# Ten expert slabs instead of eight, two of them on lent space

## The reference, cut to what matters

```python
h = layer_norm(ALPHA * h + mixed, ln_g[i, 0], ln_b[i, 0])
ffn = hierarchical_moe(h, ...)      # 32 experts, the best 2 per token
h = layer_norm(ALPHA * h + ffn, ln_g[i, 1], ln_b[i, 1])
# an expert: (silu(xb @ w_gate[e]) * (xb @ w_up[e])) @ w_down[e]
```

## Time and profile before

| what | us |
|---|---|
| median of 3 runs (2404.62 to 2407.61) | 2405.11 |
| the profiled execution's own time | 2405.83 |
| its span | 2404.1 |
| PE busy | 2144.1 (89%) |
| DVE busy | 736.6 (31%) |
| ACT busy | 515.1 (21%) |
| POOL busy | 301.3 (13%) |

### The profile page before, as it was taken

How to read it: one execution, slowest core, us unless ns; L and a number is a source line. 1 busy time by engine, 2 the same in 40 slices (tenths; PEclk the granted TensorE clock), 3 DMA queues, 4 the chain that set the end, 5 groups by cost and what they waited for, 6 DMA issues and landing times. The chain is left out here.

```text
span 2404.1 us, 28333 instructions
## 1 busy us (share of the span) xinstructions
PE 2144.1 (89%) x11502; PEld 1232.8 (51%) x11502; DVE 736.6 (31%) x1587; ACT 515.1 (21%) x1193; POOL 301.3 (13%) x309
## 2 busy tenths in 40 slices
PE   4999989999999999868999999959996899999991
PEld 2446644444444578345555455547754555455550
DVE  5054235342665445452111011042125211101104
ACT  1123221021554144212221121130001122112110
POOL 0000000212232211101111111022000111111101
PEclk9999988999999999978999999979997899999996
DMA  9315243042003121138999999971133899999992
GB/s 346 107 58 176 75 153 110 30 158 70 1 1 109 70 73 54 54 122 333 421 423 424 423 423 423 418 280 52 72 114 112 337 422 422 424 423 422 424 407 116
DMA packets 100567, 545.88 MB, mean 227 GB/s; under 512 B 13296, under 2 KB 27417, under 8 KB 66490
## 3 DMA queue, kind: packets, MB, share of 16 engines
q1 hardware_dynamic: 79238, 493.55, 50.8%
q0 software_dynamic: 20320, 48.01, 5.6%
q10 hardware_dynamic: 868, 2.38, 0.3%
HBM read 538.79 MB, written 28.94 MB: 236 GB/s over the span
## 5 line engine op out<-in xcount | busy, mean ns | idle before, releaser
L721 PE MATMUL ps<-arena,ring 128*128 128x512 f32 (+11 forms) x2000 | 608.0, 463 | 10.3 <-ACT arena L1349 3.0
L721 PEld LDWEIGHTS ps<-arena,ring 128*128 128x128 f32 (+3 forms) x2000 | 358.4, 190 | 247.7 <-issue 205.1
L1141 PE MATMUL ps<-ring,arena 128*64 128x256 f32 x3648 | 410.0, 382 | 2.3 <-DMA ring<-in_moe_w_up_dram 1.3
L1141 PEld LDWEIGHTS ps<-ring,arena 128*64 128x64 f32 x3648 | 257.5, 137 | 134.3 <-issue 3.0
L802 PE MATMUL ps<-ring,arena 128*128 128x512 f32 (+1 forms) x560 | 250.7, 605 | 6.5 <-DVE arena L2007 4.2
L1154 PE MATMUL ps<-ring,arena 128*64 128x512 f32 x896 | 210.8, 614 | 22.8 <-DMA ring<-in_moe_w_down_dram 22.8
L2157 DVE SCALAR_TENSOR_TENSOR arena<-arena,ps 128x256 f32<-128x256 f32 x78 | 32.9, 421 | 565.9 <-ACT arena L1541 565.9
L2417 POOL DMA_INDIRECT assignment_rows<-arena x78 | 82.1, 1052 | 827.4 <-ACT arena L1547 802.9
L802 PEld LDWEIGHTS ps<-ring,arena 128*128 128x128 f32 (+1 forms) x560 | 102.9, 187 | 141.3 <-issue 141.0
L1141 PE MATMUL ps<-arena 128*64 128x256 f32 x1344 | 151.1, 380 | 0.0
L1154 PEld LDWEIGHTS ps<-ring,arena 128*64 128x64 f32 x896 | 65.7, 142 | 135.6 <-issue 102.2
(11 more groups left out here) (299 smaller groups left out, 1826.2 us busy)
## 6 DMA issues: line engine op xcount, KB each, us to landing
ring<-in_moe_w_gate_dram SPq DMA_DIRECT2D x48, 2048.0 KB
ring<-in_moe_w_up_dram SPq DMA_DIRECT2D x48, 2048.0 KB
ring<-in_moe_w_down_dram SPq DMA_DIRECT2D x48, 2048.0 KB
arena<-in_moe_w_gate_dram SPq DMA_DIRECT2D x16, 2048.0 KB
arena<-in_moe_w_up_dram SPq DMA_DIRECT2D x16, 2048.0 KB
arena<-in_moe_w_down_dram SPq DMA_DIRECT2D x16, 2048.0 KB
ring<-in_ada_w_dram SPq DMA_DIRECT2D x12, 2048.0 KB
ring<-in_a_w_in_dram SPq DMA_DIRECT2D x12, 1536.0 KB
```

The lines of the kernel that those rows point to most:

```text
L721: ins = pe.matmul(dst, w, m, start=i == 0, stop=i == len(pairs) - 1)
L1141: ins = pe.matmul(ps[CAP * i:CAP * (i + 1), bank_, 256 * j:256 * (j + 1)], rows_t[:, k, :], w[:, k, 256 * i:256 * (i + 1)], start=k == 0, ...
```

## The change

Two more slab places, slots 8 and 9, are made out of the first 8192 columns of `arena`. These hold X (5120 columns), and the norm rows `lnp` (2048) and `gate_b` (1024) which are moved there; HT and all behind it move up by 3072 columns. The expert turns go round ten places instead of eight, starting with the ring, then HT's place, the mixer's, then slots 8 and 9. Turns of experts past position 22 skip slots 8 and 9; their last users are turn 58 (down of expert 18) and turn 59 (gate of expert 20). SP waits for `h_out` (X is in DRAM) ahead of turn 8.

X is read back from `h_rows` by POOL after scatter 30 (LENT_BACK is 30), 2.1 MB, followed by the gain and bias for alpha (1.05 MB). Alpha moves from the blocks 1 to 5 to the blocks 32 to 36 and waits for both reads (`x_lent`, `lnp_in`). The loads `load_lnp(2)` and `load_lnp(4)` ahead of the stages go away. The load of the next norm's rows moves from scatter 10 to behind scatter 38, the last one.

```diff
 RING = 6
-SLABS = 8
+SLABS = 10
 SLAB = 4096
+LENT = (8, 9)
+LAST_LENT = 22
...
-    for n, (kind, l, _) in enumerate(STREAM):
+    for n, (kind, l, at_) in enumerate(STREAM):
         if kind == "expert":
-            i = n - TURN[("expert", l, (0, 0))]
-            cycle = [(ring_at + j) % RING for j in range(RING)] + list(range(RING, SLABS))
-            s = cycle[i % SLABS]
+            if n == TURN[("expert", l, (0, 0))]:
+                cycle = deque([(ring_at + j) % RING for j in range(RING)] + list(range(RING, SLABS)))
+            while cycle[0] in LENT and at_[0] > LAST_LENT:
+                cycle.popleft()
+            s = cycle[0]
+            cycle.rotate(-1)
...
+LENT_BACK = sum(s <= LAST_LENT for s, _ in BLOCKS) + 1
...
-        arena = sb("arena", [P, 24576])
-        lnp = sb("lnp", [P, 2, D])
-        gate_b = sb("gate_b", [P, D])
+        arena = sb("arena", [P, 27648])
+        lnp = arena[:, 5120:7168].rearrange("p (i d) -> p i d", d=D)
+        gate_b = arena[:, 7168:8192]
...
-        HT = at(5120, DC * TM).rearrange("p (c t) -> p c t", t=TM)
-        R0 = 9344
+        HT = at(8192, DC * TM).rearrange("p (c t) -> p c t", t=TM)
+        R0 = 12416
...
-            return ring[:, s * SLAB:(s + 1) * SLAB] if s < RING else at((5120, R0 + 8192)[s - RING], SLAB)
+            return ring[:, s * SLAB:(s + 1) * SLAB] if s < RING else at((8192, R0 + 8192, 0, 4096)[s - RING], SLAB)
...
                     if turn == first + RING + 1:
                         sp.wait_ge(*((yT_ready, DC) if l == 0 else (comb_done, COMBINED[(3, 3)] + 1)))
+                    if turn == first + RING + 2:
+                        sp.wait_ge(h_out, 16 * (5 if l == 0 else 9))
...
                 for n in range(NBS):
                     hidden(NBS * l + n)
                     hidden_copy(NBS * l + n)
-                    if 1 <= n < (6 if l == 0 else 5):
-                        alpha(l, n - 1)
+                    if 0 <= n - LENT_BACK - 2 < (5 if l == 0 else 4):
+                        alpha(l, n - LENT_BACK - 2)
...
             def alpha(l, t):
 
                 r, x = rows_of(t), X[0:rows_of(t), t, :]
-                vec.wait_ge(h_out, 16 * (5 if l == 0 else 9))
+                vec.wait_ge(x_lent, 32 if l == 0 else 48)
...
                 affine(1, t)
-            load_lnp(2)
...
-                    if n == 10:
+                    if n == LENT_BACK:
+                        for s in LENT:
+                            pool.wait_ge(*consumed(max(t for t in range(len(STREAM)) if SLOT[t] == s and STREAM[t][1] == l)))
+                        pool.dma_start(X[:, 0:NT, :], h_d[l][0:S, :].rearrange("(t p) d -> p t d", p=P)).then_inc(x_lent, 16)
+                        if l == 0:
+                            pool.dma_start(X[0:META, 4, :], h_d[l][S:TM, :]).then_inc(x_lent, 16)
+                        load_lnp(2 + 2 * l)
+                    if n == NBS - 1:
                         pool.wait_ge(alpha_done, 5 if l == 0 else 9)
                         load_lnp(3 + 2 * l)
...
             combined(0, (4, 0, 1, 2, 3))
-            load_lnp(4)
```

More of the change, by code:

```diff
@@ L9 @@
+from collections import deque
 from contextlib import ExitStack
@@ L157 @@
 SLOT, USE, PREV = place_slabs()
-assert 3 * NE % SLABS == 0
 PROWS = {}
@@ L298, in build @@
         spec = sb("spec", [P, 64])
-        expert_of = arena[:, 24528:24560]
+        expert_of = arena[:, 27600:27632]
         group_of = sb("group_of", [P, NE])
         negm = sb("negm", [P, GROUPS, NT, HPG])
-        den = arena[:, 24448:24448 + GROUPS * NT * HPG].rearrange("p (g t h) -> p g t h", g=GROUPS, t=NT)
+        den = arena[:, 27520:27520 + GROUPS * NT * HPG].rearrange("p (g t h) -> p g t h", g=GROUPS, t=NT)
         nmax = sb("nmax", [P, 8])
         dsum = sb("dsum", [P, 8])
[L305 to L308, removed]
+        slot_tok = arena[:, 26832:26832 + NBLK].bitcast(I32)
+        half_id = arena[:, 26896:26896 + NBLK].bitcast(I32)
+        pair_tok = arena[:, 26952:26952 + NPR].bitcast(I32)
+        row_cols = arena[:, 26972:26972 + 4 * DC].rearrange("p (l i c) -> p l i c", l=2, i=2)
         key_bias = sb("key_bias", [P, NE])
@@ L313, in build @@
         over_i = sb("over_i", [1, NOVER + 1], I32)
-        gates = arena[:, 24560:24570].rearrange("p (k t) -> p k t", k=2)
+        gates = arena[:, 27632:27642].rearrange("p (k t) -> p k t", k=2)
         ps = ctx.enter_context(nc.psum_tensor("ps", [P, 8, 512], F32))
@@ L395, in build @@
         cnt = at(RT + 1120, 4 * NE).rearrange("p (n e) -> p n e", e=NE)
-        key, rank, heavy, base_of, need, over_at = (at(23936 + NE * i, NE) for i in range(6))
-        need_i = at(23936 + NE * 6, NE).bitcast(I32)
-        rank_i = at(24160, 5 * NE).bitcast(I32).rearrange("p (t n) -> p t n", n=NE)
+        key, rank, heavy, base_of, need, over_at = (at(27008 + NE * i, NE) for i in range(6))
+        need_i = at(27008 + NE * 6, NE).bitcast(I32)
+        rank_i = at(27232, 5 * NE).bitcast(I32).rearrange("p (t n) -> p t n", n=NE)
         row_of = at(R0, 10).rearrange("p (t k) -> p t k", k=2)
@@ L439, in build @@
         rot_in = sem("rot_in")
+        x_lent = sem("x_lent")
         x_in, meta_in, x_back, x1_out, x1_back = (sem(n) for n in ("x_in", "meta_in", "x_back", "x1_out", "x1_back"))
```

## The result

The kernel got slower: 2424.45 us as the median of 4 runs (2419.81 to 2427.45) against 2404.86 (4 runs of before, 2404.62 to 2407.61), a ratio of 1.0076 (95% interval 1.0064 to 1.0088). I had said 2402. The profiled execution has a span of 2425.7 us, 21.6 more than before; it was the slowest of the four.

A forecast was written before the change was run, and what follows sets the result against it. Slab landings were taken to bound both expert stages, with gains only in the dry stretch ahead; -1.4 (first stage) + 0.3 (tail) - 2.1 (second stage) = -3.2 us gave 2402 us, range 2395 to 2412.

The forecast's parts named there:

- What bounds the kernel: Both expert stages: the last slab's landing sets the end; only the dry stretch ahead of the full one can be won.
- part 1 (the lead): Stage starts: two more slabs fill the dry stretch, a lead of 9.9 us, or 9.1 and 8.2 us.
- Part 2 (the gathers get company): Stage starts: slabs 8 and 9 delay the first gather and PE's start by 2.8 us, at most 4.7.
- hardly held up: Rival at stage starts: gathers wait 1.5 us instead of 2.8; time 2399, or 2395 at the bound; chance 0.27.
- Part 3 (X through the full stretch): Full stretch of each stage: reading X back costs 5.1 us in the first and 5.0 us in the second.
- Part 4 (the wait of alpha): Block 32: reads land 33.5 us behind scatter 30; first stage still ends 1.4 us earlier, second 2.1 us.
- X comes back late: Rival at alpha's block 32 wait: slower POOL reads take 37.5 us, together +13 us, 2418; chance 0.20.
- Part 5 (the tails): Behind the last scatters: next norm's rows issued there may delay reads 0 to 1.5 us, taken as 0.3.
- The other rivals: Gathers held up by the full 4.7 us: 2406, chance 0.10; too few slab places at the end: 2420, chance 0.05.
- Eight places at the end: Rival after turn 60: eight places are too few, loads wait and the lead is lost; +15 us, 2420; chance 0.05.
- four signs of being wrong: Gathers under 5 or over 7 us, alpha over 36 us behind scatter 30, slab hole after turn 60, PE-paced stage end.

The follow-up runs named there:

- e8: Changed kernel, but SP waits for the stage's first two gathers ahead of turn 8 and X is not read back; 2389.20 us, ratio 0.9927.
- e7: Changed kernel with eight slabs as before; X stays in place but is still read back and waited for; 2427.26 us, ratio 1.0087.
- e5: Changed kernel, but SP waits for the first two gathers ahead of turn 8 and itself reads X ahead of turn 70; 2400.07 us, ratio 0.9977.
- e2: Changed kernel, but SP instead of POOL reads X back, in the slabs' queue ahead of turn 70; 2411.12 us, ratio 1.0018.
- e3: Changed kernel with alpha two blocks later, at blocks 34 to 38, reads still on POOL's queue; 2411.85 us, ratio 1.0024.
- e6: Changed kernel without the read-back of X; alpha works on what slots 8 and 9 left; 2400.71 us, ratio 0.9978.
- e4_small: Changed kernel, but turns 8 and 9 are read in 2 KB instead of 16 KB pieces, one expert's weight rows misordered; 2416.30 us, ratio 1.0041.

## Why the prediction was wrong, step by step

**What bounds the kernel** and **part 1 (the lead)** were right. The hole of 9.1 and 8.2 us was there, and the lead alone measured 17.6 us (e8), with 17.3 for the two holes and 19.8 for four slabs.

**Part 2 (the gathers get company)** was the first step that failed, in size. I took 2.8 us (my own terms, 3.3 and 3 less 3.7, give 2.6) and gave 4.7 as the upper bound; it was 6.9 and 5.9. The bound came from one gather in the full stretch, and from the moved bytes of its window, not from its landing. POOL's queue from 1957 to 1972 us in the kernel before:
```profile
q0 software_dynamic: 224, 0.37, 6.5%
```
These are the scatter's 80 packets and the gather's 144. By 1967 all the bytes had moved but only 213 of the packets; the last one came behind 1968, so 8.4 us was no upper bound. That gather also ran beside smaller packets: the slabs' had 9.8 KB from 1957 to 1967 (389 packets, 3.80 MB) and 14.6 KB at the start of the changed kernel's stage. I had read the one-for-one packets of the earlier trace rows and used them, but counted only the 66 real rows: 4.1 packets per engine where a gather has 9. By terms: the 3 us to the first bytes were 4.3, the 3.3 us for moving were 5.1, and 1.2 us from the last packet to PE's start stood in no term; together 10.6 where I had 6.5. So the rival that I called "hardly held up" had the mechanism of one half right, with the wrong count. The Trainium skill ("DMA: Bandwidth & Descriptors", section on queues, rings and completion order) says that an engine takes turns packet by packet; the trace agrees with 203 to 230 packets, and the small ones have to be counted as well.

**Part 3 (X through the full stretch)** was right: 10.1 forecast, 9.6 measured, or 12.1 by the other pair.

**Part 4 (the wait of alpha)** failed most: about 0.6 us in the sum, 14.0 measured. Two of its terms were off. The first is the time of the reads. X and its vectors were there 39.3 and 38.2 us behind scatter 30 (39.5 and 38.8 in e7) where I had 33.5. POOL's queue in the changed kernel from 1484.5 to 1501 us, then from 1501 to 1515.85, when alpha starts:
```profile
q0 software_dynamic: 461, 1.89, 28.4%
q0 software_dynamic: 408, 1.26, 21.9%
```
In the first stretch my price held, 0.115 MB per us against 0.113. In the second the queue moves as many packets per us (27.5 against 27.9) but only 0.085 MB, because more of the packets are small: 137 of both queues' are under 512 bytes, against 39 before. I had priced bytes where the queue is paced by packets, which is the count missed in part 2 again. Scatters send such packets (80 each, of 64 rows, when one is alone in the queue); no run isolates whose packets all the small ones are. The second term is the lead at scatter 30, 5.3 us instead of 9.6 (1481.87 to 1476.53), since part 2 had eaten most of the rest and the stage's first gather itself was issued 1.4 us later in this execution. Block 33's transposes then stand at 1519.3 instead of my 1509.3, and of 14.0 us PE could take back the 5.3 us of the earlier trace rows: +8.7, and +10.0 were measured. What remains is the last block's 0.7 us of waiting for DVE and a lower clock when PE starts again behind 11.6 us of standing idle (mean granted clock 0.70 from 1519 to 1525 us, part of it at the lower level, and 1.00, the full 2.4 GHz, from 1525): without waits PE needs 58.5 us for the rest of the stage, before 57.8. I had written that the margin was nothing and that each us beyond 33 counts, so the mechanism was the second rival's, "X comes back late", at 39 us instead of 43. It should have had the larger chance. A margin of zero with an uncertain read time is no forecast of no cost: lateness costs 1 us each, earliness gains nothing.

**Part 5 (the tails)** was near: behind the first stage 1.8 us came back (its +10.0 had become +8.3 at the second stage's first gather), where I had +0.3; behind the second 1.2 were lost.

**The other rivals.** Eight places at the end are enough: e5 gives up slots 8 and 9 at the same turn and moves 422 GB/s from 1130 to 1550 us. The changed kernel's 417 hold a dip to 322 and 300 GB/s from 1519 to 1525 and to 1530, right behind the time in which PE waited for DVE and freed no slab. The range of 2395 to 2412 was too low because the bound of part 2 and the price of part 4 were both too low. Three of my four signs of being wrong showed: gathers over 7 us, alpha more than 36 us behind scatter 30, and stage ends that PE's own pace sets. The fourth, a hole in the slab queue after turn 60, is this dip at most.

## What to carry to other kernels

Space that is lent has to be paid back, and the waiter should stand well behind the landing: moving either the read to the slabs' own queue, or the waiter by two blocks, took 12 to 14 us off. A transfer that shares the engines is to be counted in packets, the empty rows' too, and not in bytes alone. And before a dry stretch of the queue is filled, look what small transfer lies in it on the way to the first matmul: filling it some 14 us later (turn 8 15.4 us behind turn 7 instead of 1.1) gave 14 us back, and the lead alone was still worth its 17.6 us (e8).

## What the runs showed of the hardware that was not expected

- A gather of 128 rows beside 2 MB loads in 16 KB pieces took 10.2 to 10.9 us to PE's start (changed kernel, e2, e3, e6, both stages), 7.0 and 7.8 us beside 2 KB pieces, and 3.4 to 5.3 us where the loads were not in flight behind it.
- A gather sends 144 packets, however many of its 128 rows are empty: 720 for five, with 1.58 MB, in three kernels.
- The first packet of POOL's queue comes 1.7 us behind the gather's issue with the slab queue about to run dry, 4.3 us beside 16 KB pieces and 4.6 us beside 2 KB pieces (first stage).
- Both queues move the same number of packets while both are full: 329 to 328 from 1485 to 1497 us and 191 to 192 from 1092.3 to 1099.5 in the changed kernel. The 925 to 296 of e4_small hold 4.6 us without any packet of POOL's; counted from its first packet (1088.66 to 1092) they are 388 to 296.
- 3.15 to 3.21 MB through POOL's queue beside the slabs take 38 to 40 us from the scatter ahead of them to the waiter, in both stages of two kernels (changed kernel, e7), in 968 to 987 packets of that queue.
